# Residual rows and early loads requested ahead of the barrier, and the spread in two groups on four banks

## The reference, cut to what matters

```python
for i in range(DEPTH):                      # 2 layers
    h = h + mixer_i(rms_norm(h, ...))       # delta rule, then dilated attention
    h = h + hierarchical_moe(rms_norm(h, ffn_norm[i]), ...)
    h = h + per_layer_embedding(h, p[i], ple_norm[i], w_ple_gate[i], w_ple_proj[i])

# hierarchical_moe: 4 groups x 8 experts, each token goes to 2 experts of one group
hdn = jax.nn.silu(xb @ w1[e]) * (xb @ w3[e])    # 1024 -> 512, xb: the rows of expert e
out = out.at[row_tok].add((hdn @ w2[e]) * row_w[:, None])
# per_layer_embedding
sigmoid(rms_norm(h, g) @ w_gate) * (p_i @ w_proj)
```

## Time and profile before

| what | value |
|---|---|
| median of 3 executions | 1733.32 us (1730.41 to 1734.15) |
| profiled execution, from its first to its last instruction | 1731.8 us; the page gives no other time of it |
| feed-forward part, layer 0: barrier to the last expert product | 402 to 872 us |
| feed-forward part, layer 1: the same | 1190 to 1659 us |
| moved by DMA | 481.59 MB, mean 278 GB/s |

### The profile page before, as it was taken

One profiled execution on the slowest core, in us unless ns is written; L12 is line 12 of the kernel. 1 busy time (PEld: TensorE's weight loads), 2 busy tenths in 40 slices (PEclk: granted clock), 3 DMA queues, 4 the chain that ended last, 5 costly groups with the idle time before them and its releaser, 6 DMA issues. The chain is left out here.

```text
span 1731.8 us, 20065 instructions
## 1 busy us (share of the span) xinstructions
PE 1677.2 (97%) x7380; PEld 806.9 (47%) x7380; DVE 710.0 (41%) x1514; ACT 452.4 (26%) x693; POOL 140.0 (8%) x192
## 2 busy tenths in 40 slices
PE   7999999998999999998999999998999999999898
PEld 4555566644334344343355564554343443434343
DVE  4778455515334343342333113365243443434241
ACT  5767233313010010101034716653110101101020
POOL 0026620001000000000000101100000000000000
PEclk9999999999999999999999999999999999999999
DMA  8121432286999999999991010058999999999950
GB/s 289 52 73 38 130 86 73 99 349 227 408 427 427 426 427 425 427 428 427 422 345 49 1 74 32 1 199 320 366 427 427 427 425 427 427 427 428 427 195 38
DMA packets 89355, 481.59 MB, mean 278 GB/s; under 512 B 22721, under 2 KB 39873, under 8 KB 62657
## 3 DMA queue, kind: packets, MB, share of 16 engines
q1 hardware_dynamic: 84672, 472.16, 67.3%
q0 software_dynamic: 4608, 8.40, 1.3%
HBM read 476.86 MB, written 12.06 MB: 282 GB/s over the span
## 5 line engine op out<-in xcount | busy, mean ns | idle before, releaser
L2158 PE MATMUL bank<-ring,xT 128*64 128x512 f32 x2040 | 460.7, 598 | 17.3 <-DMA ring<-in_w 16.4
L2094 DVE TENSOR_TENSOR H<-H,bank 128x512 f32<-128x512 f32 x240 | 154.0, 683 | 295.8 <-PE bank L2145 295.8
L2158 PEld LDWEIGHTS bank<-ring,xT 128*64 128x64 f32 x2040 | 140.1, 137 | 280.9 <-issue 264.8
L2195 PE MATMUL bank<-ring,sg 128*64 128x512 f32 x1008 | 223.4, 595 | 1.7 <-issue 1.2
L2195 PEld LDWEIGHTS bank<-ring,sg 128*64 128x64 f32 x1008 | 70.4, 137 | 131.0 <-issue 125.1
L705 PE MATMUL bank<-ring,ring 128*128 128x512 f32 x256 | 130.0, 604 | 0.0
L690 PE MATMUL bank<-ring,ring 128*128 128x512 f32 x256 | 112.9, 593 | 0.0
L2651 PE MATMUL bank<-ring,ring 128*128 128x512 f32 x256 | 110.5, 592 | 0.0
L2248 ACT ACTIVATE sg<-bank 128x512 f32<-128x512 f32 x32 | 19.2, 599 | 348.1 <-PE bank L2169 348.1
L2145 PE MATMUL bank<-high,Sb 128*128 128x512 f32 x240 | 106.7, 445 | 0.0
L2084 DVE SCALAR_TENSOR_TENSOR low<-bank,weight_now,high 128x512 fp32r<-128x512 f32 x60 | 45.1, 751 | 135.5 <-ACT high L2259 132.5
(11 more groups left out here) (346 smaller groups left out, 1985.1 us busy)
## 6 DMA issues: line engine op xcount, KB each, us to landing
ring<-in_w SPq DMA_DIRECT2D x178, 2048.0 KB, 28.6
ring<-in_w_heads SPq DMA_DIRECT2D x16, 1024.0 KB, 5.4
ring<-in_w SPq DMA_DIRECT2D x10, 1024.0 KB, 9.3
ring<-in_w SPq DMA_DIRECT2D x18, 512.0 KB, 7.4
ring<-in_w_ple_gate SPq DMA_DIRECT2D x4, 2048.0 KB, 28.7
ring<-in_w SPq DMA_DIRECT2D x4, 1536.0 KB, 8.2
ring<-in_w_kv SPq DMA_DIRECT2D x3, 2048.0 KB, 20.4
ring<-in_b_w_q SPq DMA_DIRECT2D x3, 2048.0 KB, 19.4
```

The costliest lines, as they stand in the source:

```text
L2094: dve.tensor_tensor(out, out, k.bank[6 + j % 2][:, :], ALU.add).then_inc(s.added, 1)
L2158: last = pe.matmul(out[e * SLOTS:(e + 1) * SLOTS, :], k.xT[:, at, e * SLOTS:(e + 1) * SLOTS], rows, start=(at == 0), stop=(at == DC - 1))
L2195: last = pe.matmul(k.bank[2 + n][e * SLOTS:(e + 1) * SLOTS, :], k.hT[:, c, e * SLOTS:(e + 1) * SLOTS], w[:, e, :], start=(c == 0), stop=(c ...
```

## The change

Five things are done:

1. The rows stored for the gather are those of `H` itself, not normed ones. `store_rows` is called at the end of the mixer, a tile as soon as it has its last addition. The scale `rstd` is put back later: it goes through the lookup matmul in three bf16 parts (`aux` has 11 columns for 8), a new reduction gives `slot_rstd`, the Silu takes it as its scale, and the token weight is multiplied by it once. The four scalings to `xn` are gone.
2. The squares of the norm are written to `y` and `product`, so `ring2[:, 1]` is free. Piece 1 of pair 1 is asked for at the end of the mixer, in one piece, when the last matmul of the mixer is done.
3. The inputs of `p_i @ w_proj` (now three loads at once) and the rest of pair 0 are asked for at the end of the mixer. Their tiles are laid out where the mixer has nothing. The weights of `first_half` now lie in `xg`, and so the gather waits for the fourth `first_half` product (`r.product`, 4).
4. The spread of a pair runs in two groups of four tiles: behind piece 1 and behind piece 3, in four banks (6, 7, 2, 3), ahead of `expert_turn`; both turns of the gathered rows follow `expert_turn`.
5. VectorE's order follows: additions 0 to 3, the hidden product, additions 4 to 7, both evacuations of the turned rows. `expert_down` waits for addition 5, since banks 2 and 3 are its own.

The core of the diff:

```diff
         if m == 3:
-            sp.dma_start(k.early_quarter[:, :], upper(m, src)).then_inc(landed, 16)
+            sp.dma_start(k.early_quarter[:, :], upper(m, src)).then_inc(k.s_early, 16)
         if m == 5:
...
 
     load_expert_pair(k, layer, 0, load)
+
+
+def load_products(sp, k, layer):
+
+    sp.dma_start(k.early_p.inputs, k.p_t[layer].rearrange("(p c) n -> p c n", c=2)).then_inc(k.s_p, 16)
+    for half, memory in enumerate((k.early_p, k.early_second_p)):
+        sp.dma_start(memory.weights, w_proj_half(k, layer, half)).then_inc(k.s_p, 16)
+
+
+def store_rows(sp, k, layer, tiles, settled):
+
+    for t in tiles:
+        sp.wait_ge(*settled[t])
+        sp.dma_start(k.rows[layer][t * P:(t + 1) * P, :], k.H[:, t, :]).then_inc(k.s_rows, 16)
 
 
...
@@ -1824,14 +1837,12 @@
 
     gain = k.g_ffn[:, layer, :]
     for t in range(0, NT, 2):
-        squares_scalar(act, k, s, t)
+        wait(act, s.ss, t // 2)
+        squares_scalar(act, k, s, t, k.y[:, :])
         raw_chunk_scalar(act, k, s, t + 1, gain, DC)
     deviation(act, k, s)
     for c in range(5, DC, 2):
         raw_chunk_scalar(act, k, s, c, gain, DC)
-    act.wait_ge(s.rstd, 1)
-    for t in range(1, NT, 2):
-        act.activation(k.xn[:, t, :], k.H[:, t, :], ACT.Copy, scale=k.rstd[:, t:t + 1]).then_inc(s.xn_odd, 1)
     act.wait_ge(s.sums, 1)
     act.wait_ge(s.cleared, 1)
...
     variance(dve, k, s, NT // 2, NT // 2)
     raw_chunk_vector(dve, k, s, 4, gain, DC)
     inverse_deviation(dve, k, s)
     raw_chunk_vector(dve, k, s, 6, gain, DC)
     dve.wait_ge(s.rstd, 1)
-    for t in range(0, NT, 2):
-        dve.tensor_scalar(k.xn[:, t, :], k.H[:, t, :], k.rstd[:, t:t + 1], None, ALU.mult).then_inc(s.xn, 1)
+    ch = s.chain = Chain(dve, s.steps)
+    split_deviations(dve, k, ch)
     dve.wait_ge(s.sums, 1)
     odd = slice(ODD, ODD + LOGITS)
     dve.tensor_copy(k.by_expert[odd, :], k.bank[1][odd, :]).then_inc(s.odd, 1)
...
 
+def split_deviations(dve, k, ch):
+
+    parts = k.aux[:, :, :, RSTD:PARTED]
+    ch.link(dve.tensor_copy(parts[:, :, :, 0], bcast(k.rstd[:, :], 2, PAIRS)))
+    ch.link(dve.tensor_tensor(k.gs[:, :], k.rstd[:, :], parts[:, :, 0, 0], ALU.subtract))
+    ch.link(dve.tensor_copy(parts[:, :, :, 1], bcast(k.gs[:, :], 2, PAIRS)))
+    ch.link(dve.tensor_tensor(parts[:, :, :, 2], bcast(k.gs[:, :], 2, PAIRS), parts[:, :, :, 1], ALU.subtract))
+
+
 def route_pool(pool, k, s):
 
...
     dve.wait_ge(s.eexp, 1)
     ch.link(dve.scalar_tensor_tensor(k.gs[:, :], k.e2[:, :], 1.0, k.gs[:, :], ALU.add, ALU.mult))
     ch.link(dve.reciprocal(k.c1[:, :], k.gs[:, :]))
+    ch.link(dve.tensor_tensor(k.c1[:, :], k.c1[:, :], k.rstd[:, :], ALU.mult))
     ch.link(dve.tensor_tensor(k.c2[:, :], k.c1[:, :], k.e2[:, :], ALU.mult))
     ch.link(dve.tensor_tensor(k.oh1[:, :, :], k.oh1[:, :, :], bcast(k.c1[:, :], 2, EXPERTS), ALU.mult))
...
 def weigh_slots(dve, k, s, pair, i):
     dve.wait_ge(s.weighed, i + 1)
+    dve.tensor_reduce(k.slot_rstd[:, bass.ds(pair, 1)], k.bank[5][:, RSTD - WEIGHT:PARTED - WEIGHT], AX.X, ALU.add)
     for e in range(2):
         half = slice(e * SLOTS, (e + 1) * SLOTS)
...
-def add_results(dve, k, s, i, js):
+def spread_bank(j):
+
+    return (6, 7, 2, 3, 2, 3, 6, 7)[j]
+
+
+def add_results(dve, k, s, i, js, alone=False):
 
     for j in js:
         n, t = j // NT, j % NT
         dve.wait_ge(s.spread, 8 * i + j + 1)
         out = k.H[:, t, n * HALF:(n + 1) * HALF]
-        dve.tensor_tensor(out, out, k.bank[6 + j % 2][:, :], ALU.add).then_inc(s.added, 1)
+        bank = 6 + j % 2 if alone else spread_bank(j)
+        dve.tensor_tensor(out, out, k.bank[bank][:, :], ALU.add).then_inc(s.added, 1)
 
 
...
-        last.then_inc(s.spread, 1)
+def spread_matmuls(pe, k, s, j, bank):
+
+    n, t = j // NT, j % NT
+    for m, part in enumerate(parts_of(k, n)):
+        last = pe.matmul(bank[:, :], k.Sb[:, t * P:(t + 1) * P], part, start=(m == 0), stop=(m == 1))
+    last.then_inc(s.spread, 1)
+
+
+def spread_first(pe, k, s, i):
+
+    pe.wait_ge(s.Sb, i + 1)
+    pe.wait_ge(s.low, 2 * i + 2)
+    wait(pe, s.added, 8 * i)
+    for j in range(NT):
+        spread_matmuls(pe, k, s, j, k.bank[spread_bank(j)])
+
+
+def spread_second(pe, k, s, i):
+
+    for j in range(NT, 2 * NT):
+        if j < NT + 2:
+            pe.wait_ge(s.added, 8 * i + j - 1)
+        spread_matmuls(pe, k, s, j, k.bank[spread_bank(j)])
...
-    if not alone:
+    if not (alone or first):
         wait(pe, s.low, 2 * i)
+        pe.wait_ge(s.added, 8 * i - 2)
     for c in range(FC):
         slot = 4 + c // 2
...
 
-def activate_hidden(act, k, s, i, alone=False):
+def activate_hidden(act, k, s, i, pair, alone=False):
 
     act.wait_ge(s.h1, i + 1)
     if not alone:
         wait(act, s.hidden_turned, i)
-    act.activation(k.h[:, :], k.bank[0][:, :], ACT.Silu).then_inc(s.silu, 1)
+    act.activation(k.h[:, :], k.bank[0][:, :], ACT.Silu, scale=k.slot_rstd[:, bass.ds(pair, 1)]).then_inc(s.silu, 1)
     act.wait_ge(s.hidden_turned, i + 1)
     act.activation(k.hT[:, :, :], k.bank[0][:, :].rearrange("p (c n) -> p c n", c=FC), ACT.Copy).then_inc(s.hT, 1)
...
-            spread(pe, k, s, i - 1, (0, 1))
+            spread_first(pe, k, s, i - 1)
         expert_up(pe, k, 1, 0, memory, k.bank[1], s.half2, arrived)
-        if not first:
-            spread(pe, k, s, i - 1, (2, 3))
+        if first:
+            pe.wait_ge(k.s_early, 16 * 3 * (layer + 1))
         expert_up(pe, k, 1, 1, memory, k.bank[1], s.h3, arrived, apart=k.early_quarter if first else None)
         if not first:
-            spread(pe, k, s, i - 1, (4, 5))
+            spread_second(pe, k, s, i - 1)
+        expert_turn(pe, k, s, i)
         if not last:
             turn_rows(pe, k, s, i + 1, 0)
-        expert_turn(pe, k, s, i)
-        if not first:
-            spread(pe, k, s, i - 1, (6, 7))
-        if not last:
             turn_rows(pe, k, s, i + 1, 1)
         if not last:
             expert_down(pe, k, s, i, memory, arrived, first=first)
 
     pe.wait_ge(r.places, 1)
     identify_tokens(pe, k, s, 0, 0)
-    first_half(pe, k, r, (3,))
+    first_half(pe, k, r, layer, (3,))
     early_second(pe, k, r)
     pe.wait_ge(r.parts, 1)
...
-            add_results(dve, k, s, i - 1, (4, 5))
+            add_results(dve, k, s, i - 1, range(NT, 2 * NT))
         if not last:
             evacuate_rows(dve, k, s, layer, i + 1, 0)
-        if not first:
-            add_results(dve, k, s, i - 1, (6, 7))
+            evacuate_rows(dve, k, s, layer, i + 1, 1)
         mark_tokens(dve, k, s, i, i)
-        if not last:
-            evacuate_rows(dve, k, s, layer, i + 1, 1)
         if not (last or second_last):
             build_slots(dve, k, s, i + 2, i + 2)
...
 
 
 def experts_fetch(pool, k, s, r, layer):
 
-    pool.wait_ge(r.stored, 16 * NT)
-    pool.wait_ge(r.blank, 1)
+    pool.wait_ge(k.s_rows, 16 * NT * (layer + 1))
+    pool.wait_ge(r.product, NT)
     fetch_rows(pool, k, s, layer, 0)
     with pool.Fori(1, PAIRS) as i:
...
 
-    def load_around_fetch(m, src):
-
-        if m == AROUND:
-            slot = piece_slot(1, m)[0]
-            sp.wait_ge(r.stored, 16 * NT)
-            for half in (slice(0, 2048), slice(2048, 4096)):
-                if half.start:
-                    sp.wait_ge(s.xg, 16)
-                sp.dma_start(slot_memory(k, slot)[:, half], src[:, half]).then_inc(landed[slot], 16)
-
-    store_rows(sp, k, r, layer)
+    sp.wait_ge(r.sums, 1)
     load_expert_pair(k, layer, 1, load_of(None, 1, (0,)))
-    load_expert_pair(k, layer, 1, load_around_fetch)
     load_expert_pair(k, layer, 1, refill_first)
     load_expert_pair(k, layer, 1, load_of(None, 1, (5,)))
     for q in range(2, TURN):
...
@@ -2772,12 +2796,9 @@
         def more(slot, src):
             sp.dma_start(slot_memory(k, slot), src).then_inc(m.landed, 16)
 
-        for dst, src in embedded(k, layer, 0):
-            sp.dma_start(dst, src).then_inc(r.p, 16)
-        load_rest_of_first(sp, k, layer, r.p)
         experts_loads(sp, k, s, r, layer)
         sp.wait_ge(*ended(s, PAIRS * PIECES - 7))
...
@@ -3022,7 +3083,12 @@
                 prefetch_shared(sp, k, 0, 5)
                 for m in (2, 3):
                     prefetch_second(sp, k, 0, m, dead)
+                load_products(sp, k, 0)
                 prefetch_experts(sp, k, 0, (0,))
+                load_rest_of_first(sp, k, 0)
+                store_rows(sp, k, 0, range(NT - 1), settled)
+                prefetch_second(sp, k, 0, 1, finished)
+                store_rows(sp, k, 0, (NT - 1,), settled)
 
             delta(k, loads, prefetch_first)
...
-                def prefetch(sp, no_keys, no_values):
+                def prefetch(sp, no_keys, no_values, finished, settled):
                     prefetch_experts(sp, k, 1, (0, 1, 2))
                     prefetch_shared(sp, k, 1, 5)
                     prefetch_second(sp, k, 1, 2, no_keys)
                     prefetch_second(sp, k, 1, 3, no_values)
```

(50 more changed lines are left out.)

156 lines of the change are left out of this document (72 added, 84 removed).

## The result

The changed kernel takes 1738.27 us (median of 20 executions, 1734.30 to 1743.11) where the kernel before takes 1733.66 (20 executions, 1730.41 to 1738.26): a ratio of 1.0031, 95% interval 1.0023 to 1.0038. It is slower by 0.3%, and the prediction of 1729.0 (1725.5 to 1732.5) is wrong in sign. The profiled execution spans 6.3 us more than before (1731.8), where the medians lie 4.6 us apart; TensorE (PE) is busy for 8 us less in it.

A forecast was written before the change was run, and what follows sets the result against it. The weight stream (427 GB/s) was taken as the bound, so slot 1's refill start counted: 1.83 us earlier in layer 0, 1.89 in layer 1, plus 0.5 for the clock, 4.2 together. From 1733.3 this gave 1729.0, range 1725.5 to 1732.5.

The forecast's parts named there:

- the end of the layer: Behind the last pair's piece 3: taken over as before, at no cost, with at most 0.6 us a layer as risk.
- the turn's lost cover: Last pair: `expert_turn` has no spread behind it to cover ScalarE's copy; put at nothing, else 0.6 us a layer.
- Loads ahead of the barrier: Layer heads: PE's wait for loads goes, bringing ranks 3.9 us earlier in layer 1; gain 0.8 us in layer 0.
- The barrier: Ahead of each head: SP's store of the last tile delays it by 0.55 us a layer, bounds 0 and 1.0.
- The gather's new wait: Heads: gather starts 1.0 us behind the fourth product, rows 4.35 us later; PE has them at 427.12 and 1215.43.
- The idle time before the gather: Heads: PE stands about 1.7 us for the gathered rows in both layers, without slowing what follows.
- Full rate: PE's clock behind the idle wait for gathered rows stays full; other bound 1.0 us a layer.
- The constant stretch: From slot 1's refill to the last pair's piece 3: nearly all weight stream, staying 418 to 420 us.
- The spread at nothing: Two-group spread saves PE 0.3 us a pair, 10 us over 30 pairs; costed at nothing, as late pairs wait for pieces.
- rival 1: Head's gain is eaten: gather takes 6.3 us in both layers, or barrier and clock cost 1.0 each; 1733.0, chance 0.25.
- Rival 3: Late pairs: longer PE waits drop the clock, two drops a pair costing 11 us less 4.2; 1740, chance 0.07.
- Rivals 2 and 4: PE's saving reaches the end, 1719, chance 0.07; the weight stream gets 3 us a layer shorter, 1723, chance 0.06.

The follow-up runs named there:

- e3: Kernel before, with only PE's whole program moved in memory (offset 236): 1750.22 us, ratio 1.0088 to the kernel before.
- e5: Changed kernel, each layer's expert part aligned so a code boundary lies 50 instructions behind the pair loop's end: 1731.48 us, ratio 0.9985 to the kernel before.
- e12: Repeat of e5, the well placed changed kernel, timed beside other runs on one chip: 1731.21 us, ratio 0.9993 to the kernel before.
- e8: Kernel before with its expert parts placed as in e5, nothing else changed: 1733.41 us, ratio 0.9997 to the kernel before.
- e11: Kernel before with only the new two-group spread (its turns and additions included), placed as in e5: 1733.87 us, ratio 0.9997 to the kernel before.
- e5 to e8: Besides e5 and e8: the changed kernel, placed alike, with the old spread, additions and turn order (1733.31 us), or with matmuls filling the gathered-rows wait (1731.41 us).
- e10: As e9, plus one instruction at the last pair's start announcing the branch: 1733.25 us, ratio 0.9995 to the kernel before.
- e9: Changed kernel with both expert parts placed so no code boundary lies between the pair loop's end and the branch: 1746.76 us, ratio 1.0077 to the kernel before.
- e4: Changed kernel with PE's whole program moved (offset 50) and the branch announced at the last pair's start: 1738.67 us, ratio 1.0014 to the kernel before.

## Why the prediction was wrong

**The step that failed** is the end of the layer. The sum took everything behind piece 3 of the last pair over from the trace of before and priced only the turn's lost cover (0.6 us a layer, at most). The branch to `w2` was in that trace, at 0.43 us, with a code packet 7.1 us ahead of it. That was luck of the layout: e3 is the same kernel at another place, with the wait in both layers. No term asked where PE's code lies, and none of the four rivals did. In its place the runs show 6.2 us in layer 1: 4.7 of stand and 1.5 of clock. With that put right, the direction forecast is the one measured, in e5 with an interval that excludes no change (in e12 it just includes it), and its size is about half: 2 to 3 us for 4.2. The turn's lost cover, for which 0.6 us a layer stood as the bound, cost nothing: from piece 3 to `w2` e5 takes 6.87 us, the kernel before 6.97.

**Loads ahead of the barrier.** Right where they were looked at: the wait for loads is gone in both heads, the products take 5.40 us. But in layer 1 the gain was counted from an execution that stood 2.41 us and lost 1.7 to the clock (products of 7.11 us for layer 0's 5.42, at a granted clock of 0.50). In e8's profile of the same old kernel the clock fell earlier, at the turn (0.50 from 1193 to 1195 us), and the products, which came later by that, wait for nothing and take 5.40; in e3's the turn takes 3.79 us, the wait is 0.77 and the products take 5.42:

```profile
1190.94 5.47 PE L359 MATMUL bank<-consts,H 128*128 128x128 f32 x32 [1.97 <-PEq L2919]
...
1201.75 5.40 PE L1742 MATMUL bank<-product,xT 128*128 128x512 f32 x12
```

```profile
1206.88 5.42 PE L1743 MATMUL bank<-product,xT 128*128 128x512 f32 x12 [0.77 <-DMA early_piece<-in_w]
```

So this term (3.9 us of the head of layer 1, 1.9 behind the gather) was mis-sized from one execution. In layer 1 of the four profiles with the old loads the wait is 0 to 2.4 us, and in e8, e5 and e12, where it is gone, the clock still falls once in that head, to 0.50, at the turn.

**The barrier.** PE stood 1.74 and 2.02 us in it, 0.36 and 0.32 more than before, for the 0.55 that was taken: right within its bounds.

**The gather's new wait.** In layer 1 the fourth product ends at 1209.5 and the rows are turned at 1214.47, 4.9 us later (forecast 1.0 + 4.35): the gather starts at 1210.42 and its rows are there 4.05 us after that. Right within 0.4. The prediction's text has one sign wrong: in layer 0 the product's end, 422.02, lies 0.4 us behind the old start of the gather, 421.65, not ahead of it. Its sum uses the times themselves and doesn't suffer.

**The idle time before the gather.** 1.63 and 1.41 us, for 1.7. "Full rate" held in layer 0 (first piece 3.65 us) and not in layer 1 (5.35): the bound of 1.0 us a layer was too small, it is 1.7. Together with the 5.41 us of the turn behind the barrier (3.79 before), the clock, 0.50 from 1190 to 1192 us and 0.54 from 1218 to 1220, took 3.3 us in that head. So slot 1 was refilled 36.4 us behind the turn's start in layer 1, for the 33.5 forecast (1224.59 less 1190.51 and the barrier's 0.55).

**The constant stretch.** From that refill to piece 3 of the last pair, layer 0 took 420.09 us, for 420.0; layer 1 took 420.46, for 418.8. Right in kind, 1.7 us off. Most of that is scatter between executions: over both layers of all 14 profiles the stretch takes 418.5 to 421.4 us. In the mean it is 420.2 in the 12 layers whose first piece took more than 3.65 us, at a mean granted clock of 0.68 to 0.83, and 419.7 in the other 16, at 1.00. So the 0.5 us that the sum took back for the clock fits, within an error of some 0.3, and the clock does not account for the 1.7.

**The spread at nothing.** Right for the spread alone (e11): the waits of `expert_up` for pieces grew from 16.4 to 25.9 us instead (26.5 in the changed kernel).

**Rivals.** Of rival 1 the gather's part is not seen (4.2 and 4.05 us from its start to the rows, not 6.3), the clock's part is, in layer 1 and above its bound. Rival 3, the clock, was the right mechanism at other places, the head of layer 1 and the branch, not the late pairs: their waits grew to 1.7 us at the longest, and from 1500 to 1640 us the clock stays at 1.00. Rivals 2 and 4 are not seen.

**The range.** Its upper end does not follow from its own bounds: 1733.3 less the least gain of 0.3 us is 1733.0, which is rival 1's time and already above 1732.5.

## What to carry to other kernels

A long branch over code that hardly ever runs is a timed part of a tuned kernel, here at 0.32 to 0.47 us or at 6.08 to 6.21: an edit that changes the number of instructions on that engine moves it against the code packets, 256 instructions each here, and the one miss of the changed kernel cost 6.2 us, more than the 4.2 that the whole edit was to bring. Look for a branch of some us and for the code packets around it before explaining a small loss by data. Compare versions with such branches announced or aligned, or a difference of 6 to 8 us for each of them may be the layout's (16.5 us for the two of e3). And a wait or a lowered clock that one profiled execution shows is no fixed term of a sum, unless a second one shows it at the same place.

## What the runs showed of the hardware

- The branch of PE at the end of a layer took 6.08 to 6.21 us in all eight cases without a code packet between the loop's end and the branch, with the DMA queues full of weights, and 0.32 to 0.47 us in the other 20, which had one; in the eight the next packet started 3.5 to 3.6 us behind the branch's start.
- Where a boundary was passed some 125 instructions ahead of the branch, the packet came 10.9 to 12.7 us ahead of it, in each of the six runs placed so (e5 to e8, e11, e12); some 50 instructions ahead was too few in the two cases profiled.
- PE ran the second pass of its loop, 1434 to 1466 instructions or some 92 to 94 KB at the packets' 64 bytes each, without new code: in none of the 14 profiles did a code packet start later than 1.3 us into it.
- With one instruction that announces the branch, the packet came 11.5 us ahead of it in both layers at the bad place (e10; none came in e9, without it), but none came where a boundary lay between (e4's layer 0, a branch of 6.21 us).
